# First attention of a two-block forward pass: queries moved to the partitions, a running product in place of exp, ln and suffix-sum matmuls

## The reference, cut to what matters

```python
z = jnp.einsum('bhqd,bhkd->bhqk', qb, kb) * inv_sqrt_d
mask = kpos < qpos
log_beta = jax.nn.log_sigmoid(z)
log_1m_beta = jnp.where(mask, log_beta - z, 0.0)
suffix = lax.cumsum(log_1m_beta, axis=3, reverse=True) - log_1m_beta
a = jnp.where(mask, jnp.exp(log_beta + suffix), 0.0)
out = jnp.einsum('bhqk,bhkd->bhqd', a.astype(vb.dtype), vb)
```

## Time and profile before

| | us |
|---|---|
| median of 3 runs | 3103.62 |
| lowest and highest run | 3098.84, 3111.96 |
| span of the profiled execution | 3091.5 |
| PE busy in it | 2909.7 (94%) |
| DVE, ACT, POOL busy | 1508.1, 945.4, 943.4 |

### The profile page before, as it was taken

How to read it: one execution, slowest core, us unless ns; L and a number is a source line. 1 busy time by engine, 2 the same in 40 slices (tenths; PEclk the granted TensorE clock), 3 DMA queues, 4 the chain that set the end, 5 groups by cost and what they waited for, 6 DMA issues and landing times.

```text
span 3091.5 us, 35185 instructions
## 1 busy us (share of the span) xinstructions
PE 2909.7 (94%) x13227; PEld 2331.4 (75%) x13227; DVE 1508.1 (49%) x2270; ACT 945.4 (31%) x1871; POOL 943.4 (31%) x703
## 2 busy tenths in 40 slices
PE   3899999799999999999899999898998999999997
PEld 3688878587786666667688888777886888888886
DVE  5666566632205888874520006775526431451444
ACT  4200001413216787852401007653114110110112
POOL 1233323132234444433233344111332333333321
PEclk7999999899999999999999999898999999999999
DMA  5344444363523333331245125112111111111111
GB/s 194 102 141 144 138 130 143 116 204 123 182 84 96 82 82 82 82 96 48 89 143 191 52 58 164 42 42 82 48 48 41 48 48 48 48 48 48 48 47 70
DMA packets 271510, 287.80 MB, mean 93 GB/s; under 512 B 15043, under 2 KB 216172, under 8 KB 269420
## 3 DMA queue, kind: packets, MB, share of 16 engines
q1 hardware_dynamic: 261580, 241.50, 26.0%
q10 hardware_dynamic: 9760, 44.04, 3.6%
HBM read 228.88 MB, written 56.62 MB: 92 GB/s over the span
## 4 chain that ended last, share of the span: by engine, by line
PE 82%; DVE 9%; ACT 4%; DMA 2%; issue 2%; SPq 0%; POOL 0%; DVEq 0%; ACTq 0%; POOLq 0%
PE PS L1255 63%; PE PS L463 3%; PE PS L1287 3%; PE PS L468 2%; PE PS L600 2%; DVE s_sp L808 1%; DMA mod_raw<-in_w_ada 1%; DVE M L1740 1%; PE PS L569 1%; PE PS L560 1%; PE PS L590 1%; DVE M L1779 1%; PE PS L482 1%; PE PS L1315 1%; DVE s_al L820 1%
## 5 line engine op out<-in xcount | busy, mean ns | idle before, releaser
L1255 PE MATMUL PS<-opA,w_hi 128*128 128x512 f32 x4736 | 1475.7, 392 | 27.3 <-POOL w_lo L1128 11.8
L1255 PEld LDWEIGHTS PS<-opA,w_hi 128*128 128x128 f32 x4736 | 894.7, 189 | 217.2 <-issue 17.1
L1255 PE MATMUL PS<-opA,w_lo 128*128 128x512 f32 x2368 | 925.6, 391 | 0.0
L1123 POOL CAST w_hi<-w_raw 128x1024 fp32r<-128x1024 f32 (+1 forms) x193 | 204.1, 1057 | 1447.9 <-PE PS L1255 1384.6
L1128 POOL TENSOR_TENSOR w_lo<-w_raw,w_hi 128x1024 fp32r<-128x1024 f32 (+1 forms) x198 | 479.3, 2421 | 200.3 <-ACT w_hi L1517 184.8
L1255 PEld LDWEIGHTS PS<-opA,w_lo 128*128 128x128 f32 x2368 | 448.0, 189 | 92.7
L1255 PE MATMUL PS<-opB,w_hi 128*128 128x512 f32 x1216 | 377.9, 391 | 4.4 <-DVE opB L1964 3.4
L1255 PEld LDWEIGHTS PS<-opB,w_hi 128*128 128x128 f32 x1216 | 229.0, 188 | 53.3 <-DVE opB L1964 3.8
L1740 DVE SCALAR_TENSOR_TENSOR M<-mod_raw,small,M 128x512 f32<-128x512 f32 x168 | 186.3, 1109 | 147.7 <-DMA mod_raw<-in_w_ada 70.2
L1255 PE MATMUL PS<-opB,w_lo 128*128 128x512 f32 x608 | 237.2, 390 | 0.0
L1975 DVE SCALAR_TENSOR_TENSOR X<-PS,mod,X 128x512 f32<-128x512 f32 x96 | 72.1, 751 | 290.8 <-PE PS L1255 285.1
(11 more groups left out here) (179 smaller groups left out, 3420.7 us busy)
## 6 DMA issues: line engine op xcount, KB each, us to landing
mod_raw<-in_w_ada SPq DMA_DIRECT2D x96, 256.0 KB, 2.9
w_raw<-in_w_up SPq DMA_DIRECT2D x44, 512.0 KB, 3.8
w_raw<-in_w_in SPq DMA_DIRECT2D x34, 512.0 KB, 3.8
w_raw<-in_a_w_in SPq DMA_DIRECT2D x32, 512.0 KB, 4.8
q_dram<-stage ACTq DMA_DIRECT2D x16, 1024.0 KB, 4.0
hin<-q_dram SPq DMA_DIRECT2D x64, 256.0 KB, 5.5
k_dram<-stage ACTq DMA_DIRECT2D x13, 1024.0 KB, 4.8
mod_raw<-in_b_mod_w SPq DMA_DIRECT2D x48, 256.0 KB, 2.8
```

The costliest lines, as they stand in the source:

```text
L1123: pool.tensor_copy(hi, raw).then_inc(pool_done, 1)
L1255: ins = pe.matmul(ps, w[:, k0 + k, :], rhs(part, k0 + k), start=(k == 0 and n == 0), stop=(k == chunks - 1 and n == 2))
```

## The change

The stage is turned round. The queries lie on the partitions. A head is 8 items, n = 8 h + i: query block i of 128 against its i + 1 key blocks, so 128 to 1024 columns wide. PE forms the scores (`scores`), ACT takes two sigmoids from them, `rest` of -z and `beta` of z. DVE runs a product along the keys backwards over `rest` (`stick_scan`, one `tensor_tensor_scan` in place with the same tensor as both inputs). POOL multiplies `beta` by it, shifted by one key (`stick_a`). PE transposes the result block by block (`turn`), in pieces of up to four blocks: p = 0 and, for i of 4 and more, p = 1. The high part is copied out of PSUM by ACT, and by DVE for piece 1 of i = 6 and 7 (`hi_on_dve`); DVE subtracts for the low part (`stick_lo`). After odd i, PE multiplies by the values for the pair of query blocks i - 1 and i (`values`). A half head is finished by ACT and DVE (copy, add), and after odd heads by three instructions on POOL (`finish`), which were on DVE. `turn` and the splits run three items behind the scores, `values` four, the finish five. SP now issues all head loads before the weights of unit `U_BOUT + 2`, since `rest` lies in the space of weights, and reloads `X` after the last `values`.

```diff
--- before.py
+++ after.py
@@ -90,15 +90,21 @@
...
-LAG_B, LAG_A, LAG_H, LAG_V = 3, 4, 5, 6
-RING = (0, 1, 2, 3, 6, 7)
+TURN_LAG, VALUE_LAG, OUT_LAG = 3, 4, 5
+BETAS, FACTORS = 4, 3
...
@@ -233,19 +239,14 @@
...
+        beta = [at(f"beta{i}", AT_X + 4 * KIB * i, [T]) for i in range(BETAS)]
+        a_hi = [at("a_hi0", AT_M, [6, 2 * P], F32R), at("a_hi1", AT_X + 16 * KIB, [8, 2 * P], F32R)]
+        a_lo = [at("a_lo0", AT_M + 6 * KIB, [6, 2 * P], F32R), at("a_lo1", AT_X + 24 * KIB, [8, 2 * P], F32R)]
...
+        rest = [at("rest0", AT_W, [T]), at("rest1", AT_W + 12 * KIB, [T]), at("rest2", AT_W + 20 * KIB, [T])]
...
@@ -425,78 +426,81 @@
...
+        def stick_kbs(c):
+            n, p = STICK_PIECES[c]
+            return range(NQ * p, min(NQ * p + NQ, n % NT + 1))
+        def hi_on_dve(c):
+            n, p = STICK_PIECES[c]
+            return p == 1 and n % NT >= 6
...
+            def scores(n):
...
+                if n >= 2:
+                    pe.wait_ge(act_done, at("stick_beta", n - 2))
+                for k0 in range(0, (i + 1) * P, HALF):
+                    width = min(HALF, (i + 1) * P - k0)
+                    z = PS[:, 2 * (n % 2) + k0 // HALF, 0:width]
+                    k = hin[:, s, 0, k0:k0 + width]
+                    last = k0 + width == (i + 1) * P
+                    pe.matmul(z, hin[:, s, 1, i * P:(i + 1) * P], k, start=True, stop=False)
+                    ins = pe.matmul(z, hin[:, s, 2, i * P:(i + 1) * P], k, start=False, stop=True)
+                    if last:
+                        ins = pe.matmul(z[:, width - P:width], ident_r[:], mask_r[:], start=False, stop=True,
+                                        skip_group_check=True)
...
+            def turn(n):
+                pe.wait_ge(pool_done, at("stick_a", n))
+                for p in range(n % NT // NQ + 1):
+                    c = STICK_PLACE[n, p]
+                    if c >= 2:
+                        pe.wait_ge(dve_done, at("stick_lo", c - 2))
+                    for kb in stick_kbs(c):
+                        ins = pe.transpose(PS[:, 4 + c % 2, (kb - NQ * p) * P:(kb - NQ * p + 1) * P],
+                                           beta[n % BETAS][:, kb * P:(kb + 1) * P], ident[:])
...
+            def values(n):
...
+                s, o, g = h % 2, 6 + i // NQ, i // 2
+                q0 = (i - 1) % NQ * P
+                pe.wait_ge(dve_done, at("stick_lo", STICK_PLACE[n, i // NQ]))
+                if h and i % NQ == 1:
+                    pe.wait_ge(dve_done, at("stick_o", h - 1, i // NQ))
+                for kb in range(i + 1):
+                    cols_of = slice(P if kb == i else 0, 2 * P)
+                    dst = PS[:, o, q0 + cols_of.start:q0 + 2 * P]
+                    v = hin[:, s, 3, kb * P:(kb + 1) * P]
+                    pe.matmul(dst, v, a_hi[g % 2][:, kb, cols_of], start=(kb == 0), stop=False, skip_group_check=True)
+                    ins = pe.matmul(dst, v, a_lo[g % 2][:, kb, cols_of], start=False, stop=(kb == i),
...
-                ins = pe.matmul(scores_of(g, qs), tri[:], s_sp[:, g % 3, qs:], start=False, stop=True,
...
-                    ins = pe.matmul(scores_of(g, qp), nones[:], s_p[:, (g - 1) % 3, qp:], start=False, stop=True,
...
+                if i == NT - 1:
+                    names[("stick_free", h)] = names[("stick_v", n)]
...
+            pe.wait_ge(dve_done, at("v_split", U_QZ - 1))
+            for n in range(STICK_ITEMS + VALUE_LAG):
+                if n < STICK_ITEMS:
+                    scores(n)
+                if 0 <= n - TURN_LAG < STICK_ITEMS:
+                    turn(n - TURN_LAG)
+                if n >= VALUE_LAG and (n - VALUE_LAG) % 2:
+                    values(n - VALUE_LAG)
...
@@ -628,57 +632,50 @@
...
+            for n in range(STICK_ITEMS + OUT_LAG + 1):
+                if n < STICK_ITEMS:
+                    w = (n % NT + 1) * P
+                    z = banks(2 * (n % 2))[:, 0:w]
+                    act.wait_ge(pe_done, at("stick_s", n))
+                    if n < FACTORS:
+                        act.wait_ge(x_out, at("x_out", 0))
+                        act.wait_ge(pool_done, at("split", U_BOUT))
...
-                    act.activation(s_t[:, g % 3, qs:], scores_of(g, qs), ACT.Abs).then_inc(act_done, 1)
...
-                    act.activation(s_t[:, e % 3, qs:], s_t[:, e % 3, qs:], ACT.Exp, scale=-1.0).then_inc(act_done, 1)
...
-                    act.activation(s_a[:, e % 3, qs:], scores_of(e, qs), ACT.Exp).then_inc(act_done, 1)
...
-                    act.activation(s_t[:, e % 3, qs:], s_t[:, e % 3, qs:], ACT.Ln, bias=1.0).then_inc(act_done, 1)
...
+                        act.wait_ge(pool_done, at("stick_a", n - FACTORS))
+                    act.activation(rest[n % FACTORS][:, 0:w], z, ACT.Sigmoid, scale=-1.0).then_inc(act_done, 1)
+                    step(act_done, "stick_rest", n)
+                    if n >= BETAS:
+                        act.wait_ge(pe_done, at("stick_T", STICK_PLACE[n - BETAS, (n - BETAS) % NT // NQ]))
+                    act.activation(beta[n % BETAS][:, 0:w], z, ACT.Sigmoid).then_inc(act_done, 1)
+                    step(act_done, "stick_beta", n)
+                m = n - TURN_LAG
+                if 0 <= m < STICK_ITEMS:
+                    for p in range(m % NT // NQ + 1):
+                        c = STICK_PLACE[m, p]
+                        if hi_on_dve(c):
+                            continue
+                        kbs = stick_kbs(c)
+                        act.wait_ge(pe_done, at("stick_T", c))
+                        if m >= 4:
+                            act.wait_ge(pe_done, at("stick_v", (m - 4) | 1))
+                        dst = a_hi[m % NT // 2 % 2][:, kbs[0]:kbs[-1] + 1, m % 2 * P:m % 2 * P + P]
+                        src = PS[:, 4 + c % 2, 0:len(kbs) * P].rearrange("p (k q) -> p k q", q=P)
+                        act.activation(dst, src, ACT.Copy).then_inc(act_done, 1)
+                        step(act_done, "stick_hi", c)
+                e = n - OUT_LAG
+                if 0 <= e < STICK_ITEMS and e % NQ == NQ - 1:
...
@@ -766,67 +763,46 @@
...
-                    dve.scalar_tensor_tensor(out=s_sp[:, e % 3, qs:], in0=scores_of(e, qs), scalar=0.0,
-                                             in1=s_t[:, e % 3, qs:], op0=ALU.max, op1=ALU.add).then_inc(dve_done, 1)
...
-                    dve.tensor_copy(s_ah[:, e % 3, qs:], s_a[:, e % 3, qs:]).then_inc(dve_done, 1)
...
-                    dve.tensor_tensor(s_al[:, e % 3, qs:], s_a[:, e % 3, qs:],
...
+                dve.wait_ge(act_done, at("stick_tmp", h, hf))
+                dve.tensor_tensor(s_o[main, hf, :], PS[main, 6 + hf, :], s_o[main, hf, :], ALU.add).then_inc(dve_done, 1)
+                step(dve_done, "stick_o", h, hf)
+            for n in range(STICK_ITEMS + OUT_LAG + 1):
+                if n < STICK_ITEMS:
+                    w = (n % NT + 1) * P
+                    f = rest[n % FACTORS]
+                    dve.wait_ge(act_done, at("stick_rest", n))
+                    dve.tensor_tensor_scan(f[:, 0:w][:, ::-1], f[:, 0:w][:, ::-1], f[:, 0:w][:, ::-1], 1.0, ALU.mult,
+                                           ALU.bypass).then_inc(dve_done, 1)
+                    step(dve_done, "stick_scan", n)
+                m = n - TURN_LAG
+                if 0 <= m < STICK_ITEMS:
+                    for p in range(m % NT // NQ + 1):
+                        c = STICK_PLACE[m, p]
+                        kbs = stick_kbs(c)
+                        g = m % NT // 2 % 2
+                        at_q = slice(m % 2 * P, m % 2 * P + P)
+                        src = PS[:, 4 + c % 2, 0:len(kbs) * P].rearrange("p (k q) -> p k q", q=P)
+                        hi = a_hi[g][:, kbs[0]:kbs[-1] + 1, at_q]
+                        if hi_on_dve(c):
+                            dve.wait_ge(pe_done, at("stick_T", c))
+                            dve.wait_ge(pe_done, at("stick_v", (m - 4) | 1))
+                            dve.tensor_copy(hi, src).then_inc(dve_done, 1)
+                            step(dve_done, "stick_hi", c)
+                            dve.wait_ge(dve_done, at("stick_hi", c))
+                        else:
+                            dve.wait_ge(act_done, at("stick_hi", c))
+                        dve.tensor_tensor(a_lo[g][:, kbs[0]:kbs[-1] + 1, at_q], src, hi.bitcast(F32),
+                                          ALU.subtract).then_inc(dve_done, 1)
+                        step(dve_done, "stick_lo", c)
+                e = n - OUT_LAG
+                if 0 <= e < STICK_ITEMS and e % NQ == NQ - 1:
+                    finish(e)
...
@@ -1024,8 +1000,10 @@
...
                 sp.wait_ge(x_out, at("x_out", n))
-                sp.wait_ge(dve_done, at("att_end", n))
-                sp.wait_ge(dve_done, at("att_end2", n))
...
+                    sp.wait_ge(pe_done, at("stick_v", STICK_ITEMS - 1))
+                else:
+                    sp.wait_ge(dve_done, at("att_end", n))
                 for j in range(KC):
...
```

(35 more changed lines are left out.)

214 lines of the change are left out of this document (33 added, 181 removed).

## The result

The changed kernel takes **3124.02 us** (median of 20 runs, 3110.11 to 3150.16) against 3109.89 for the kernel before (20 runs, 3098.84 to 3124.3, on the same chip): ratio 1.0047, 95% interval 1.0027 to 1.0067. It is 14 us slower; the forecast said 48.

The account below looks back on a forecast made before the run. PE, busy 94%, was taken to bound the kernel. Turns 25.7, finish 0.3 and PE lateness 3.0 make 29.0 a head, 464 for 16, plus 9.5: 473.5 against 425.4, +48, 3152 us; range 3060 to 3190.

Parts of the forecast that it names:

- The 12.1 us added for what lies around the span: Whole kernel: difference between profiled span and median, added to the 3139.5 us span to give 3152.
- the price of POOL's products: POOL, first attention: eight products a head at 0.15 + 0.28 W us (W key blocks), 11.3 us a head.
- Fill and drain: Ends of the first attention: fill as before, longer path behind the last product, 9.5 us in all, bounds 7 and 12.
- The scans: DVE: running products taken as two passes, 0.15 + 0.27 W us (W key blocks), 10.9 us a head.
- Scan and product exclude each other: DVE and POOL at SBUF: scan counted as two-input, taking turns with POOL's product, together 22.2 us a head.
- Rival 2: DVE scan does not exclude POOL's product; DVE alone sets the pace, 24.1 us a head, 3074 us; chance 14%.
- PE's turn: PE: scores behind values delay scans at i = 4 and i = 2; 3.0 us a head taken, 6.0 at 1.2 GHz.
- Rival 4: PE falls to 1.2 GHz for the whole stage: 32 us a head, stage 521.5, 3200 us; chance 12%.
- The finish: POOL: 3.1 us a head of finishing work, mostly in POOL's idle time; 0.3 counted, bounds 0 and 3.1.
- PE off the limit: PE, first attention: work falls from 25.3 to 12.8 us a head, so PE stops binding, busy half to three quarters.
- Nothing else in the program changes: Rest of the kernel: everything outside the changed first attention keeps its time, no us added.
- Rivals 1, 3 and 5: Stage: turns pack, PE warm, 3104, 15%; one-pass scan excluding POOL, 3089, 9%; one-pass scan not excluding POOL, 3008, 5%.

Follow-up runs that it names:

- e11: Changed kernel with POOL's product over all w keys, without the one-key shift and with inputs swapped: first attention 459.8 us, median 3128.2 us, one execution.
- e2: Changed kernel with the two sigmoids swapped on ACT and scores held in PSUM until the scan: first attention 460.8 us, ratio 1.0081 to before.
- e3: e2 with the scan's unused second input read from PSUM instead of SBUF: first attention 418.4 us, ratio 1.0007 to the kernel before.
- e4: Changed kernel with PE's scores issued one item further ahead, before the values: first attention 396.2 us, ratio 0.9930 to the kernel before.
- e6: Changed kernel with POOL's three finish instructions on 8 columns instead of 512: first attention 426.1 us, median 3108.37 us, one execution.
- e10: Changed kernel with DVE's scan replaced by a one-pass elementwise squaring: first attention 392.1 us, median 3075.09 us, one execution.

## Why the forecast had the direction and not the size

The forecast's likeliest case was slower by 48; measured is slower by 14, less than the 15.5 us that the forecast would have called no change. The mechanism was right in the main, and the size was not. Point by point, by its own steps:

- **The stage and its sum.** 29.0 a head and 9.5 of fill and drain were forecast, 473.5. The trace has 27.3 and 4.6, 441.4. The 32 us between them are 16 x 1.7 = 27 and 4.9. The 12.1 us added for what lies around the span were wrong (3145.07 stands beside a span of 3143.2, 1.9 apart; before's profiled execution was merely a short one), but they stood on both sides and cancel in the 48.
- **The step that failed: the price of POOL's products, 11.3 a head.** I took it from the weight split, which reads both inputs at the same place. The products of a head are 0.41, 0.64, 0.86, 1.09, 1.31, 1.54, 1.77 and 2.00 by the changed kernel's timeline: 9.6, which is 1.7 less. Not all of it counts: in the forecast's own sum the splits are longer than the products of i = 0 to 2, and at i = 4 the scan waits for PE and not for the product of i = 3. The products of i = 4 to 7 were taken at 7.9 and take 6.6: 1.3 a head, 20 us. e11 puts nearly the forecast's price back and takes 459.8, 18 us more. So this term is worth 18 to 20 of the 27 us. The other 7, 0.4 a head, are spread over several steps, and no run takes them apart.
- **Fill and drain, 9.5 (bounds 7 and 12), was the second.** It is 4.6, under the lower bound, and by two errors against each other. Rows of DVE in the first and in the last head:

```profile
960.45 2.98 DVE L780 TENSOR_TENSOR_SCAN rest<-rest 128x1024 f32<-128x1024 f32 x1
```

```profile
1369.59 3.56 DVE L780 TENSOR_TENSOR_SCAN rest<-rest 128x1024 f32<-128x1024 f32 x1
```

The first head, with no splits and values of an earlier one in its way, is through its last scan 17.5 us after the start (945.91 to 963.43), where a later head takes 27.3: 9.8 saved that the forecast did not have. The end, from the last scan (1373.15) to 1387.33, takes 14.2; the forecast's product and the steps behind it are 7.4. 14.2 - 9.8 = 4.4 (4.6 with the rounded 27.3).

- **The scans, 10.9, were right.** 0.14 + 0.267 W alone. The Trainium skill, "DVE: opcode table, instruction layouts, handler registers and perf-mode slots", Datapath and trigger behaviour, says that the built-in scan runs at half throughput; the trace agrees, with 0.267 us a block of 128 columns beside 0.135 for the one-pass form of the earlier trace rows.
- **Scan and product exclude each other: right**, shown by e2 against e3, 42 us. Rival 2 would have made it 4.9 a head; e3 shows 2.6. That PE's lateness takes the rest is likely but not shown: in 1000 to 1280 us ACT waits 88.5 us for scores in e3, 79.8 in e2.
- **PE's turn: right in sum, in part by luck.** 3.7 was forecast for the path from low part to scan at i = 4, the trace has 3.73, at the full clock. 3.0 a head was taken for the lateness, a value between all at the full clock (1.2 at i = 4 and 0.2 at i = 2) and all at the lower (6.0). From the end of one scan to the end of the next the trace has 4.1 at i = 4 and 4.4 to 4.6 at i = 2, where the sum without lateness has 2.8 and 2.7: 1.3 late at i = 4 and 1.6 to 1.9, not 0.2, at i = 2, where the clock is at the lower level. Together they make 3.0 to 3.2, and e4, which moves the scores ahead in both places, gains 45 us, 2.8 a head. Rival 4, the lower clock for the whole stage, did not come (0.81), but what was said against it, that the bursts at i = 0 to 3 are dense, does not hold: the lower level stands at i = 0 and 1.
- **The finish: 0.3 a head was too little.** e6 shows 0.94.
- **PE off the limit: right**, busy 67% of the stage, forecast half to three quarters.
- **Nothing else in the program changes: right**, but with a noise that I had not counted. 493 us between the attentions and 940 behind them are the same within 1.5 us in all kernels; the second attention is not.
- **Rivals 1, 3 and 5** have nothing for them: a head of 26 at a full clock was not seen, nor a scan of 1.23. The result of 14 us is by size nearest to rival 1's no change, but by another way.

What the terms above give one by one does not add up to the difference of 32 us, because they share the same path: e4 and e10 take 45 and 49, and e4 with e3 takes no more than e4 alone, until the loads are moved as well.
